# A gated short convolution: tokens in the partitions, neighbours fetched by shifting DMAs

## The reference

```
def conv3_seq(u, w):
    up = jnp.pad(u, ((0, 0), (1, 1), (0, 0)))
    return w[0] * up[:, :-2] + w[1] * up[:, 1:-1] + w[2] * up[:, 2:]

def conv3_grid(u, w):            # GRID_W = 64
    B, L, C = u.shape
    return conv3_seq(u.reshape(B * (L // 64), 64, C), w).reshape(B, L, C)

def short_conv_mixer(h, w_in, conv_w, w_out, on_grid):
    gate_b, gate_c, hv = jnp.split(h @ w_in, 3, axis=-1)
    u = gate_c * hv
    conv = conv3_grid(u, conv_w) if on_grid else conv3_seq(u, conv_w)
    return (gate_b * conv) @ w_out
```

## Time and profile before

| | |
|---|---|
| median of 3 runs | 890.17 us (889.85 to 890.42) |
| span of the profiled execution | 888.9 us |
| PE busy | 878.5 us, 99% |
| DVE busy | 631.6 us, 71% |
| ACT busy | 460.7 us, 52% |
| POOL busy | 40.8 us, 5% |
| share of the chain that ended last, PE | 94% |
| UU, first and last product | 629.4 and 665.3 us |
| transposes of UU | 16, 272 ns each, from 633.0 us on |
| transposes of GB | 16, 271 ns each, from 644.8 us on |

### The profile page before, as it was taken

How to read it: one execution, slowest core, us unless ns; L and a number is a source line. 1 busy time by engine, 2 the same in 40 slices (tenths; PEclk the granted TensorE clock), 3 DMA queues, 4 the chain that set the end, 5 groups by cost and what they waited for, 6 DMA issues and landing times.

```text
span 888.9 us, 11084 instructions
## 1 busy us (share of the span) xinstructions
PE 878.5 (99%) x4079; PEld 732.8 (82%) x4079; DVE 631.6 (71%) x883; ACT 460.7 (52%) x697; POOL 40.8 (5%) x66
## 2 busy tenths in 40 slices
PE   9999999999999999999999999999999999999996
PEld 7878888888998888888888888888888888888885
DVE  6769987837558877688578886875768766665743
ACT  6546554626688475446535554454445344444530
POOL 0010000022103000000000000001000100000000
PEclk9999999999999999999999999999999999999998
DMA  9899999774654454454699999975755577777741
GB/s 365 346 323 352 359 363 351 270 237 145 182 175 175 162 193 164 149 186 143 218 308 348 344 329 323 333 257 163 257 179 177 182 248 241 240 233 246 250 120 47
DMA packets 94879, 215.12 MB, mean 242 GB/s; under 512 B 14520, under 2 KB 46185, under 8 KB 94697
## 3 DMA queue, kind: packets, MB, share of 16 engines
q1 hardware_dynamic: 94104, 212.97, 69.8%
q10 hardware_dynamic: 720, 1.44, 0.4%
HBM read 204.66 MB, written 9.72 MB: 241 GB/s over the span
## 4 chain that ended last, share of the span: by engine, by line
PE 94%; DMA 2%; DVE 1%; issue 1%; ACT 1%; SPq 0%; POOL 0%; POOLq 0%; DVEq 0%
PE ps L741 29%; PE ps L743 29%; PE ps L742 29%; DMA t_raw<-in_f_up 2%; PE ps L679 1%; PE ps L656 1%; PE ps L649 1%; PE ps L858 1%; PE ps L874 1%; PE ps L816 0%; PE ps L850 0%; PE ps L798 0%; DVE t_wl L1209 0%; DMA t_acc<-in_xT 0%; PE ps L865 0%
## 5 line engine op out<-in xcount | busy, mean ns | idle before, releaser
L1209 DVE TENSOR_TENSOR t_wl<-t_raw,t_wh 128x1024 fp32r<-128x1024 f32 (+3 forms) x308 | 360.4, 1203 | 103.3 <-ACT t_wh L916 102.4
L916 ACT ACTIVATE t_wh<-t_raw 128x1024 fp32r<-128x1024 f32 (+3 forms) x308 | 307.8, 1040 | 106.9 <-DMA t_raw<-in_f_up 63.3
L741 PE MATMUL ps<-t_wh,t_XH 128*128 128x512 f32 (+2 forms) x640 | 250.2, 391 | 1.3 <-DVE t_wl L1209 1.3
L743 PE MATMUL ps<-t_wh,t_XL 128*128 128x512 f32 (+2 forms) x640 | 247.1, 386 | 0.0
L742 PE MATMUL ps<-t_wl,t_XH 128*128 128x512 f32 (+2 forms) x640 | 246.8, 386 | 0.0
L741 PEld LDWEIGHTS ps<-t_wh,t_XH 128*128 128x128 f32 x640 | 120.2, 188 | 24.8 <-DVE t_wl L1209 2.1
L743 PEld LDWEIGHTS ps<-t_wh,t_XL 128*128 128x128 f32 x640 | 120.1, 188 | 24.0
L742 PEld LDWEIGHTS ps<-t_wl,t_XH 128*128 128x128 f32 x640 | 120.3, 188 | 22.9
L741 PE MATMUL ps<-t_wh,t_YH 128*128 128x512 f32 x288 | 113.1, 393 | 0.2 <-DVE t_YL L1634 0.2
L743 PE MATMUL ps<-t_wh,t_YL 128*128 128x512 f32 x288 | 112.2, 390 | 0.0
L742 PE MATMUL ps<-t_wl,t_YH 128*128 128x512 f32 x288 | 112.2, 389 | 0.0
(11 more groups left out here) (225 smaller groups left out, 614.1 us busy)
## 6 DMA issues: line engine op xcount, KB each, us to landing
t_raw<-in_f_up SPq DMA_DIRECT2D x130, 512.0 KB, 5.6
t_raw<-in_f_dn SPq DMA_DIRECT2D x66, 512.0 KB, 5.5
t_raw<-in_ada SPq DMA_DIRECT2D x48, 512.0 KB, 6.3
inner_rows<-t_tp SPq DMA_DIRECT2D x60, 128.0 KB, 3.8
t_tp<-inner_rows SPq DMA_DIRECT2D x15, 512.0 KB, 5.2
t_raw<-in_mkv SPq DMA_DIRECT2D x8, 512.0 KB, 3.6
t_raw<-in_ga SPq DMA_DIRECT2D x8, 512.0 KB, 3.3
t_raw<-in_gc SPq DMA_DIRECT2D x8, 512.0 KB, 3.2
```

The costliest lines, as they stand in the source:

```text
L741: pe.matmul(o, xh, h, start=k == 0, stop=False)
L743: x = pe.matmul(o, xl, h, start=False, stop=k == n - 1)
L916: act.activation(wh[:, m % SPL, lo:w], raw[:, n % RAW, lo:w], ACT.Copy).then_inc(hi_made, 1)
L1209: dve.tensor_tensor(wl[:, n % RAW, lo:w], raw[:, n % RAW, lo:w], wh[:, m % SPL, lo:w].bitcast(F32), ALU.subtract).then_inc(drained, 1)
```

## The change

The tokens stay in the partitions. The neighbours of a token are fetched by four DMAs of GpSimd's queue for each half of the channels, from UU into UB (the token before) and UA (the token behind), over 63 partitions each, so that a row of 64 keeps a zero at its edge; UB and UA are filled with zeros once. The taps become rows, loaded into all partitions (taps, 3 x 1024 floats) by three DMAs of GpSimd. conv_taps works on (i, t) in place of (i, j) and has five DVE instructions of 128x512, 20 in all. The gate comes from PSUM (`conv_gb`, now on DVE), and only the gated result is transposed: ACT writes YH from PSUM, DVE YL. conv_turn is gone.

The order of the groups becomes cc0, hv0, cc1, hv1, gb0, gb1. The shifts of half 0 are issued behind hv0, those of half 1 behind hv1. conv_taps of half 0 stand in the units of hv1, those of half 1 in the first two units of gb0; conv_gb(0) comes behind gb0; the gate_turns of half 0 stand in the first two units of gb1.

```diff
-    for i in (0, 1):
-        out.extend((f"conv_{n}{i}", 8, 512) for n in ("cc", "hv", "gb"))
+    out.extend((f"conv_{n}", 8, 512) for n in ("cc0", "hv0", "cc1", "hv1", "gb0", "gb1"))
...
+    wide([("conv_cc0", m) for m in range(4)], head("f2"))
+    S.extend([("load_mod", 1), ("conv_gc", 0)])
+    between = {("hv1", 0): [("conv_taps", 0, 0)], ("hv1", 1): [("conv_taps", 0, 1)], ("gb0", 0): [("conv_taps", 1, 0)],
+               ("gb0", 1): [("conv_taps", 1, 1)], ("gb1", 0): [("gate_turn", 0, 0), ("gate_low", 0, 0)],
+               ("gb1", 1): [("gate_turn", 0, 1), ("gate_low", 0, 1)]}
+    for name in ("hv0", "cc1", "hv1", "gb0", "gb1"):
+        if name == "cc1":
+            S.append(("conv_shift", 0))
+        if name == "gb0":
+            S.append(("conv_shift", 1))
         for m in range(4):
-            unit(f"conv_hv{i}", m, ahead=5)
...
+            unit(f"conv_{name}", m, *between.get((name, m), ()), ahead=5 + (name == "gb1" and m // 2))
+        S.append(({"hv": "conv_uu", "cc": "conv_gc", "gb": "conv_gb"}[name[:2]], int(name[2])))
...
+            def gate_turn(i, j):
+                b, full = place["cg", i, j]
+                ch = 4 * i + 2 * j
                 act.wait_ge(turned, full)
+                act.activation(YH[:, ch:ch + 2, :], psum_2(b), ACT.Copy).then_inc(*cg_hi.by(i, j))
...
+            def conv_taps(i, t):
+                w0, w1, w2 = (taps[:, n, half_of(i)] for n in range(3))
+                o, before, behind = GB[:, i, t, :], UB[:, t, :], UA[:, t, :]
+                if (i, t) == (0, 0):
+                    dve.wait_ge(taps_in, 48)
+                dve.wait_ge(*uu_made.at(i, t))
+                dve.tensor_tensor(o, UU[:, t, :], w1, ALU.mult).then_inc(*dve_chain.by())
+                dve.wait_ge(shifted, 64 * i + 64)
+                dve.tensor_tensor(before, before, w0, ALU.mult).then_inc(*dve_chain.by())
+                dve.tensor_tensor(behind, behind, w2, ALU.mult).then_inc(*dve_chain.by())
+                dve.wait_ge(*dve_chain.now())
+                dve.tensor_tensor(o, o, before, ALU.add).then_inc(*dve_chain.by())
+                dve.wait_ge(*dve_chain.now())
+                dve.tensor_tensor(o, o, behind, ALU.add).then_inc(*taps_made.by(i, t))
+            def conv_gb(i):
+                for t in (0, 1):
+                    o = GB[:, i, t, :]
+                    dve.wait_ge(*taps_made.at(i, t))
+                    dve.wait_ge(*tile_done(f"conv_gb{i}", t))
+                    dve.tensor_tensor(o, ps[:, bank_of(f"conv_gb{i}", t), :], o, ALU.mult).then_inc(*gb_made.by(i, t))
...
+            def load_mod(n):
+                if not n:
+                    return
+                pool.wait_ge(used, FINAL_UNIT["f2_dn1"] + 1)
+                for k in range(3):
+                    pool.dma_start(taps[:, k, :], A["taps"][k:k + 1, :].to_broadcast([P, D])).then_inc(taps_in, 16)
+                pool.memset(UB[:, :, :], 0.0).then_inc(edges_made, 1)
+                pool.memset(UA[:, :, :], 0.0).then_inc(edges_made, 1)
+            def conv_shift(i):
+                pool.wait_ge(edges_made, 2)
+                for t in (0, 1):
+                    pool.wait_ge(*uu_made.at(i, t))
+                    if i:
+                        pool.wait_ge(*taps_made.at(0, t))
+                for r in (0, 64):
+                    pool.dma_start(UB[r + 1:r + 64, :, :], UU[r:r + 63, :, :]).then_inc(shifted, 16)
+                    pool.dma_start(UA[r:r + 63, :, :], UU[r + 1:r + 64, :, :]).then_inc(shifted, 16)
```

More of the change, by code:

```diff
@@ L315, in schedule @@
     downs("f2", {}, tail)
[L317 to L324, removed]
-        for m in range(4):
-            unit(f"conv_hv{i}", m, ahead=5)
[L327 to L330, removed]
+    wide([("conv_cc0", m) for m in range(4)], head("f2"))
[8 more added lines that the diff above has]
+            S.append(("conv_shift", 1))
+        for m in range(4):
+            unit(f"conv_{name}", m, *between.get((name, m), ()), ahead=5 + (name == "gb1" and m // 2))
+        S.append(({"hv": "conv_uu", "cc": "conv_gc", "gb": "conv_gb"}[name[:2]], int(name[2])))
     late("co")
@@ L563, in build @@
         gc_made, uu_made, gb_made = (Signal(sem(n), conv_keys) for n in ("gc", "uu", "gb"))
-        ut_made, taps_made, cg_made, cg_hi, cg_lo = (Signal(sem(n), pair_keys) for n in ("ut", "taps", "cg", "cg_hi", "cg_lo"))
+        taps_in, edges_made, shifted = sem("taps_in"), sem("edges"), sem("shifted")
+        taps_made = Signal(sem("taps"), conv_keys)
+        cg_hi, cg_lo = (Signal(sem(n), pair_keys) for n in ("cg_hi", "cg_lo"))
         with_gain = Signal(sem("with_gain"), [(0, 0), (0, 1), (1, 0), (1, 1)])
@@ L881, in mturn @@
                 quad(b, hn, t, j)
[L883 to L888, removed]
             def gate_turn(i, j):
-                b = bank(("cg", i, j), *cg_made.at(i, j))
+                b = bank(("cg", i, j), *cg_lo.at(i, j))
                 for t in (0, 1):
@@ L894, in gate_turn @@
                         pe.wait_ge(*gb_made.at(i, t))
-                    pair(b, GB, t, 2 * j, t == 0)
+                    pair(b, GB[:, i], t, 2 * j, t == 0)
             part = {"mm": mm, "consts": consts_, "warm": warm, "ada_rows": ada_rows,
@@ L900, in _ @@
                     "su": su, "att_in": att_in, "att_sc": att_sc, "att_pt": att_pt, "att_val": att_val,
-                    "mturn": mturn, "conv_turn": conv_turn, "gate_turn": gate_turn}
+                    "mturn": mturn, "gate_turn": gate_turn}
             for name, *args in SCHEDULE:
@@ L1194, in _ @@
                     "sv_sq": sv_sq, "row1": row1, "att_in": att_in, "att_exp": att_exp, "att_pt": att_pt, "gate": gate,
-                    "mturn": mturn, "conv_gc": conv_gc, "conv_turn": conv_turn, "conv_gb": conv_gb,
-                    "gate_turn": gate_turn, "final": final}
+                    "mturn": mturn, "conv_gc": conv_gc, "gate_turn": gate_turn, "final": final}
             for name, *args in SCHEDULE:
@@ L1604, in conv_uu @@
                                       ALU.mult).then_inc(*uu_made.by(i, t))
[L1606 to L1622, removed]
@@ L1625, in gate_turn, with gate_low @@
+            def conv_gb(i):
[4 more added lines that the diff above has]
+                    dve.tensor_tensor(o, ps[:, bank_of(f"conv_gb{i}", t), :], o, ALU.mult).then_inc(*gb_made.by(i, t))
+            def gate_low(i, j):
                 b, full = place["cg", i, j]
-                dve.wait_ge(*taps_made.at(i, j))
-                dve.wait_ge(turned, full)
@@ L1655, in _ @@
                     "att_sc": att_sc, "att_pt": att_pt, "att_val": att_val, "gate": gate, "merge": merge,
-                    "mturn": mturn, "conv_uu": conv_uu, "conv_taps": conv_taps, "gate_turn": gate_turn, "gate_low": gate_low,
+                    "mturn": mturn, "conv_uu": conv_uu, "conv_taps": conv_taps, "conv_gb": conv_gb, "gate_low": gate_low,
                     "gained": gained, "final": final}
@@ L1952, in layout @@
         "mkn": cc(i["mem_k_norm"]), "sgb": f(i["sg_b"])[0].T,
-        "cw": np.concatenate([cc(f(i["conv_w_2"])[0, n]) for n in range(3)], 1),
         "qkg": np.pad(np.concatenate([f(i["mla_q_norm"]), f(i["mla_k_norm"])], 0).T, ((0, P - 96), (0, 0))),
@@ L1958, in layout @@
     a["cols"] = np.concatenate([parts[k] for k, _ in COLS], 1)
+    a["taps"] = f(i["conv_w_2"])[0]
     a["c"] = f(i["c_2"]).reshape(1, D)
```

35 lines of the change are left out of this document (8 added, 27 removed).

## The result

The changed kernel takes 903.83 us (median of 4 runs, 902.80 to 905.18) against 890.29 us for the kernel before in the same comparison: a ratio of 1.0143, interval 1.0131 to 1.0156, so 13.5 us slower. Forecast were 897.9 us, with a range up to 903.0. The direction and the mechanism came as forecast; the size was too small, and the time lies 0.8 us outside the range.

What follows compares the result with a forecast made beforehand. TensorE, busy 99%, was taken as the bound. Idle 7.4 + clock 2.3 - transposes 1.74 - wait 0.22 = +7.7 us: span 896.6, time 897.9; 8-in-10 range 893.5 to 903.0.

Steps and rivals of the forecast that it cites:

- D: Time from the second half's UU being written to its last shift's landing: taken as 7 us, bounds 2.5 and 12.9.
- the other 0.51 MB: Second half's shifts: bytes beyond the 0.52 MB of an earlier spill burst, at 244 GB/s left by the weight stream: 2.1 us.
- The first term: Second half's shifts: 0.52 MB priced like an earlier burst of four spill DMAs, 4.65 us, plus a little for slower start.
- D + 0.4: TensorE's idle time at gate_turn(0,0), waiting for conv_gb(0) on DVE behind the second shifts: 7.4 us.
- TensorE's arrival: TensorE reaches gate_turn(0,0), the first transpose of the gated half, after one unit of gb1, at 666.0 us.
- The floor without a landing: At gate_turn(0,0), idle time from DVE's own work even if the shifts land in under 1.8 us: 2.1 us.
- items costed at nothing: Tap loads, first half's shifts (harmless up to 13.5 us), GpSimd's co statistics, splits, second gate_turn pair: no added time.
- The clock: After the stall at gate_turn(0,0), TensorE works 4.7 us at half speed: loss 2.3 us, bounds 0 and 3.5.
- a slow queue: Rival at the shifts: landing near 12.9 us, about 3 us per GpSimd issue; +13.6 us, time 903.8; chance 0.12.
- The upper bound: For the second half's shifts: 12.9 us, the longest landing among the DMA groups in the earlier profile.
- The first, D = 4: Rival at the shifts: short landing, between 2.5 and 5.2 us; +4.7 us, time 894.9; chance 0.20.
- Rival 4: At gate_turn(0,0): DVE isn't late, tap operations at half price, landing under 5 us; -1.96 us, 888.2; chance 0.05.

Runs made afterwards that it cites:

- e12_half: Changed kernel with only UB shifted, two DMAs over 63 partitions per half, token behind left out: 898.42 us, ratio 1.0077 to the kernel before.
- e4: Changed kernel with two unshifted GpSimd copies of 512 KB per half over all 128 partitions, giving another result: 897.47 us, ratio 1.0076.
- e9: Changed kernel with four unshifted copies per half, each over 128 partitions and half of the tokens: 900.60 us, ratio 1.0101.
- e10: Changed kernel with two shifting copies per half, each over 127 partitions, border taps set to zero: 901.51 us, ratio 1.0109.
- e5: Changed kernel with four unshifted copies per half over 64 partitions each: 903.30 us (median of three), ratio 1.0136.
- e11: Changed kernel with the same four shifts per half in another order, UB's two issued before UA's two: 903.69 us, ratio 1.0136.
- e15_best63: Changed kernel's eight shifts; second half's first tap product in gb0, others behind gate_low in gb1; cc1, gb0 weights split seven units ahead: 891.04 us, ratio 0.9996.
- e2_actq: Changed kernel with the same eight shifts issued from ACT's hardware queue instead of GpSimd's: 908.71 us, ratio 1.019.
- e3_noshift: Changed kernel with no shifting DMAs and no waits for them, both neighbours left out of the result: 891.64 us, ratio 1.0005.
- e1_reorder: Changed kernel with the second half's conv_taps moved behind gate_low in gb1's first two units: 894.38 us, ratio 1.0038.
- e7_best: Changed kernel with shifts of 112 and 15 partitions, first-half taps at cc1's last unit, second-half taps at gb0's last and in gb1: 892.67 us, ratio 1.0022.
- e6_112: Changed kernel with UB and UA each shifted by one DMA over 112 partitions and one over 15, border taps zeroed: 902.10 us, ratio 1.0126.
- e8_act112: Changed kernel with shifts over 112 and 15 partitions, border taps zeroed, issued from ACT's queue: 902.14 us, ratio 1.0119.
- e14_127flat: Changed kernel with two unshifted copies per half over 127 partitions: 901.60 us, ratio 1.0116.

## Why the prediction was wrong in size

**The step that failed** is D, forecast as 7 and measured as 11.16, and in it first the term "the other 0.51 MB go at what the weight stream leaves over here, 419 less 175 = 244 GB/s: 2.1 us". It took the copies as bytes that fit into free bandwidth, at the rate of loads from HBM. But GpSimd's queue spent 4.6 us of all 16 engines on 1.03 MB, 223 GB/s, and the stream's transfers ran beside it, so that the engines were full (0.90) at 232 GB/s. With e12_half's 6.69 us for half the bytes, the other half took 4.47 us and not 2.1. The first term, 4.65 us for 0.52 MB and "a little for a slower start", was low by the rest, 6.69 instead of 4.9: it took the shorter of two bursts in the earlier trace rows. The longer one, 6.7 us, was right for this size. The measured D of 11.16 is 4.16 longer than taken and makes 3.45 of the error, since the idle time came out as D - 0.3 and not D + 0.4.

**What held.** TensorE's arrival was forecast for 666.0 and seen at 666.70, with the 0.7 us of the early stage in it. The second UU: 655.8 forecast, 656.24 seen, with the same 0.7. Five operations of taps: 3.3 forecast, 3.25 seen (645.04 to 648.29). From the landing to the end of conv_gb(0): 10.75 forecast, 678.01 - 667.40 = 10.6 seen. Across the runs idle time follows D in step:

| | e4 | e9 | e10 | changed | e5 | e11 |
|---|---|---|---|---|---|---|
| D | 7.04 | 8.57 | 9.42 | 11.16 | 12.16 | 12.74 |
| idle | 6.7 | 8.3 | 9.1 | 10.85 | 11.9 | 12.4 |

The floor without a landing was 1.3 us and not 2.1. The 16 transposes and the wait in co went; the trace of e15_best63 shows 1.75 us of the saving, its times don't. Of the items costed at nothing, the first half's shifts were not waited for at D 11, as the bound of 13.5 said, and were in e2_actq, where they took 14.85; and no second stall came at the second gate_turn. The loads of taps and the splits show no wait in the convolution; the longer waits near 60 us lie long before both.

**The clock** cost 2.86 us instead of 2.3: half speed lasted from 677.55 to about 683.4, 5.9 us of work with the transposes, where the start had 4.7. All idle times of 6.4 us (e12_half) and more were followed by the lower level. For short ones the length does not decide: behind 1.3 and 2.4 us in the convolution the clock stayed up (e3_noshift, e1_reorder), behind 1.8 it fell (e7_best); near 60 us it fell behind 1.9 us (e6_112) and stayed up behind 2.7 (e8_act112).

**The sum again**, against a forecast span of 896.6 and time of 897.9: idle +3.45, clock +0.56, early stage +0.7, and -0.3 unexplained make 901.0. The median of the runs lies 2.8 us above that span, not 1.3: 1.8 us lie between span and time of the profiled execution itself, and it was the fastest of four, 1.0 us below their median. Together 5.9 us.

**The rivals.** The second, "a slow queue", came to 903.8 and so nearest, but its mechanism was wrong: it had 3 us for each issue, and an issue takes 0.51. The upper bound, a landing of 12.9 us, was a good bound for a bad reason. The first, D = 4, is excluded by every shape tried. The Trainium skill ("DMA: Bandwidth & Descriptors", the anatomy of one DMA on the gpsimd path) makes, by the prediction's estimate, 4.4 us overlapped and 10.4 one after another; measured were 7.0 to 12.7. The changed kernel's 11.16 lies near the second, but there each copy by itself took 5.9 or 7.1 us (medians for UB and UA) from its issue to its landing, so they ran beside each other; the trace agrees with neither. Rival 4 fell: a product of two SBUF tiles takes 0.68 us.

**What explains the slow half.** The Trainium skill ("SBUF — State Buffer", Door 1: The DMA port swizzle) says that a transfer's rate depends on how many of 16 ports its partitions reach, and that partition bit 6 picks a cluster's port; partitions 0 to 63 would reach half. The traces agree as far as they go: equal packets, 32.3% of engine time against 21.3%. That ports are the reason was not tested by itself, and e11_order speaks against its simplest form: with the lower and the upper half next to each other in the queue, D was no shorter. The Trainium skill ("DMA: Bandwidth & Descriptors", Why a DMA increments its semaphore by 16) puts 127 partitions on one engine in general, and with GpSimd's queue for some direct copies on all 16; e10_127 and e14_127flat, 1.04 MB in D 9.5 us beside the stream, fit the exception.

**What stays open**: why the wait near 60 us varies; when a short idle time lets the clock fall; why 127 partitions cost more than 128; ports against another effect of the half; why the last issue on ACT's queue takes 1.80 us; why D differs by 1.6 us between the changed kernel and e11_order (11.16, 12.74).

## What to carry over

When a step begins to wait for a DMA, price the DMA in engine time next to the stream that runs there, not as bytes into spare bandwidth; on this kernel D was about twice the copies' own engine time plus 0.7 to 3.5 us on GpSimd's queue, a fit to these runs and no more. Then place everything that does not need the landing ahead of it in the waiting engine's queue, and what only a later step needs behind it: the order, with some splits made earlier, was worth 1.5% here (ratio 1.0143 to 0.9996, 13 us). The cheapest shape that still computes the convolution gave 0.3% (e10_127, 1.0109), and the cheapest of all, with another result, 0.7% (e4_whole). And a stall on TensorE can have a second price when the clock falls behind it: 2.9 us here, and 1.6 us behind a stall of 1.8.

## What the hardware showed unexpectedly

- SBUF-to-SBUF copies of 1.03 MB beside a stream take 7.0 us in two pieces over 128 partitions and 11.2 to 12.7 in four over 63 or 64; the engines' time per byte is 1.5 times as high in the latter (33.1% and 32.3% against 22.5% and 21.3% for 1.03 to 1.05 MB).
- A copy over 127 partitions costs a third more engine time than one over 128 (29.5% against 22.5%), shifted by a partition or not.
- GpSimd issues such a DMA in 0.51 us, ACT mostly in 0.73, but the last of four in 1.80 and 2.60 (e2_actq).
- From the second UU to the first packet of the copies pass 1.8 to 2.4 us on GpSimd's queue, once 3.7 (e15_best63), and on ACT's 1.6 (e2_actq) and 2.2 (e8_act112).
- The clock fell about 3 us after TensorE stopped in mid-kernel, against a little over 2 in the tail. In e7_best it fell 3.4 us after TensorE had stopped, when TensorE had been working again for 1.5 us.
